# A decoder in one program: the convolution front reordered, with X fetched in parts and the last value tiles held elsewhere

## The reference, cut to what matters

```python
def conformer_conv(h, w_pw1, b_pw1, w_dw, b_dw, ln_g, ln_b, w_pw2, b_pw2):
    u = h @ w_pw1 + b_pw1                       # 1024 -> 2048
    a, gate = jnp.split(u, 2, axis=-1)
    u = a * jax.nn.sigmoid(gate)
    u = lax.conv_general_dilated(u, w_dw[:, None, :], window_strides=(1,),
        padding=((CONV_WIDTH - 1, 0),), feature_group_count=D_MODEL) + b_dw   # 31 taps, by channel
    u = jax.nn.silu(layer_norm(u, ln_g, ln_b))
    return u @ w_pw2 + b_pw2                    # 1024 -> 1024

h = rms_norm(x, norm_mix[0])
x = x + conformer_conv(h, ...)
x = x + memory_cross_attention(rms_norm(x, norm_mem[0]), mem, w_q, w_k, w_v, w_o)
x = x + swiglu(rms_norm(x, norm_ffn[0]), w_gate, w_up, w_down)
# then: a layer with differential attention (rotary tables from `positions`, and a factor
# lambda from four small vectors), the same memory attention and feed-forward part,
# and a hybrid layer with sparse and sliding-window attention and a convolved feed-forward part
```

## Time and profile before

| | us |
|---|---|
| timed runs: median of 3 (lowest to highest) | 1323.1 (1322.09 to 1323.24) |
| profiled execution: whole | 1318.42 |
| profiled execution: span of the core | 1316.0 |
| mean granted PE clock, share of full | 0.967 |
| PE busy | 1205.4 (92% of the span) |
| DVE busy | 913.8 (69%) |
| ACT busy | 598.1 (45%) |

### The profile page before, as it was taken

One profiled execution on the slowest core, in us unless ns is written; L12 is line 12 of the kernel. 1 busy time (PEld: TensorE's weight loads), 2 busy tenths in 40 slices (PEclk: granted clock), 3 DMA queues, 4 the chain that ended last, 5 costly groups with the idle time before them and its releaser, 6 DMA issues.

```text
span 1316.0 us, 24483 instructions
## 1 busy us (share of the span) xinstructions
PE 1205.4 (92%) x9162; PEld 1138.2 (86%) x9162; DVE 913.8 (69%) x1514; ACT 598.1 (45%) x1009; POOL 96.8 (7%) x76
## 2 busy tenths in 40 slices
PE   5899979999999999998999999998977796899995
PEld 5898878999999989778999999998955586899995
DVE  5987577676665687566767666558887358899855
ACT  4655354444444432344454444443255333566541
POOL 0457100000000000000000000011000001000000
PEclk9899999999999999999999999999989788899998
DMA  7334354245555545114515554553550021355551
GB/s 264 128 114 146 125 186 167 78 173 170 187 191 192 188 165 192 64 65 160 182 61 177 189 185 170 195 186 136 179 192 7 1 96 65 130 189 188 180 207 64
DMA packets 30631, 195.27 MB, mean 148 GB/s; under 512 B 3168, under 2 KB 7392, under 8 KB 7392
## 3 DMA queue, kind: packets, MB, share of 16 engines
q1 hardware_dynamic: 30560, 194.27, 42.2%
HBM read 193.21 MB, written 1.05 MB: 148 GB/s over the span
## 4 chain that ended last, share of the span: by engine, by line
PE 76%; DVE 13%; ACT 4%; issue 4%; DMA 1%; DVEq 0%; ACTq 0%; SPq 0%
PE acc L444 19%; PE acc L446 19%; PE acc L445 19%; PE acc L474 6%; DVE wlo L1172 3%; PE acc L460 2%; DVE wlo L1167 2%; PE acc L731 2%; ACT whi L845 2%; PE st L597 1%; PE sc L507 1%; PE sc L695 1%; DVE Hlo L1200 1%; PE tp L444 1%; DMA raw<-weights 1%
## 5 line engine op out<-in xcount | busy, mean ns | idle before, releaser
L444 PE MATMUL acc<-Hhi,whi 128*128 128x256 f32 x1376 | 396.5, 288 | 13.9 <-DVE wlo L1172 13.7
L445 PE MATMUL acc<-Hlo,whi 128*128 128x256 f32 x1376 | 391.9, 285 | 0.0
L446 PE MATMUL acc<-Hhi,wlo 128*128 128x256 f32 x1376 | 391.7, 285 | 0.0
L845 ACT ACTIVATE whi<-raw 128x1024 fp32r<-128x1024 f32 x164 | 173.2, 1056 | 412.4 <-PE acc L446 383.3
L1167 DVE TENSOR_TENSOR wlo<-raw,whi 128x1024 fp32r<-128x1024 f32 x164 | 205.6, 1254 | 118.8 <-ACT whi L845 118.8
L444 PEld LDWEIGHTS acc<-Hhi,whi 128*128 128x128 f32 x1376 | 266.8, 194 | 17.8 <-DVE wlo L1172 16.0
L445 PEld LDWEIGHTS acc<-Hlo,whi 128*128 128x128 f32 x1376 | 267.0, 194 | 1.6 <-issue 1.4
L446 PEld LDWEIGHTS acc<-Hhi,wlo 128*128 128x128 f32 x1376 | 266.7, 194 | 0.0
L444 PE MATMUL acc<-FH,whi 128*128 128x256 f32 x848 | 241.6, 285 | 19.8 <-DVE wlo L1172 13.8
L446 PE MATMUL acc<-FH,wlo 128*128 128x256 f32 x848 | 240.3, 283 | 0.0
L1172 DVE TENSOR_TENSOR wlo<-raw,whi 128x1024 fp32r<-128x1024 f32 x164 | 202.8, 1237 | 1.3
(11 more groups left out here) (255 smaller groups left out, 1739.7 us busy)
## 6 DMA issues: line engine op xcount, KB each, us to landing
raw<-weights SPq DMA_DIRECT2D x180, 1024.0 KB, 4.9
MEM<-mem_in SPq DMA_DIRECT2D x2, 1024.0 KB, 10.9
cst<-consts SPq DMA_DIRECT2D x1, 1126.0 KB, 12.3
X<-x_in SPq DMA_DIRECT2D x1, 1024.0 KB, 6.1
out<-X SPq DMA_DIRECT2D x4, 256.0 KB, 2.1
PT<-positions SPq DMA_DIRECT2D x1, 128.0 KB, 14.1
cst<-consts SPq DMA_DIRECT2D x1, 32.0 KB, 1.7
```

What stands on the lines that cost most here:

```text
L444: pe.matmul(dst, w, x, start=first, stop=False)
L445: pe.matmul(dst, w, xl, start=False, stop=False)
L446: return pe.matmul(dst, wl, x, start=False, stop=last)
L845: act.activation(whi[j][:, 0:HALF, :], raw[j][:, 0:HALF, :], ACT.Copy).then_inc(hi_out, 1)
```

## The change

- SP: X comes in four parts of 256 KB with a semaphore each; tile 0 comes in two halves (`head_loaded`, then `raw_loaded[0]`); `positions` is fetched before the memory.
- ACT: a one-element activation behind the gains comes first; X's high parts follow the parts of X. The squares of X are taken in four pieces behind tile 0's high part.
- PE: pairs 0 and 1 of X are multiplied with only the first half of tile 0's low part done (`lo_head`); the second half is waited for ahead of pair 2.
- mix0 and ln_var join the norms whose squares POOL adds; PE sums two chunks for them.
- The loops over pw1 on ACT and DVE are written out. DVE does the norm ahead of the split of tile 2, and the taps stand in portions of 6, 6 and 7 behind tiles, splits and gates.
- Value tiles 6 and 7 are loaded to `held`, in the memory of Hhi and Hlo, once pw1 is done. The first two tiles of pw2 are loaded behind value tiles 4 and 5 and split ahead of and behind the LayerNorm.
- PE's mean is summed in pieces between value tiles: chunks 0 to 4 behind value tile 2, 5 and 6 behind 3, 7 behind 4.
- Constants and lambda's sums move on DVE between the splits of tile 1 and the norm; lambda and the rope angles move behind the subtraction of the mean; the two Sin activations stand ahead of the Silu.

Cut to its core:

```diff
@@ -165,7 +165,9 @@
         wlo = [sb(f"wlo{j}", [P, KC, MB], F32R) for j in range(2)]
         X = sb("X", [P, DC, S])
         SQ = sb("SQ", [P, DC, S])
-        Hhi, Hlo = sb("Hhi", [P, DC, S], F32R), sb("Hlo", [P, DC, S], F32R)
+        with ExitStack() as shared:
+            Hhi, Hlo = sb("Hhi", [P, DC, S], F32R, shared), sb("Hlo", [P, DC, S], F32R, shared)
+        held = [sb(f"held{j}", [P, KC, MB]) for j in range(2)]
         with ExitStack() as shared:
             H2 = sb("H2", [P, 2, DC, S], F32R, shared)
         H2hi, H2lo = H2[:, 0, :, :], H2[:, 1, :, :]
...
-        SUMMED = ["mem0", "ffn0", "attn1", "mem1", "ffn1", "pre2", "fpre2"]
+        SUMMED = ["mix0", "ln_var", "mem0", "ffn0", "attn1", "mem1", "ffn1", "pre2", "fpre2"]
...
-            sp.dma_start(X[:, :, :], cols(x_in)).then_inc(x_loaded, 16)
-            for j in range(2):
-                sp.dma_start(raw[j][:, :, :], weights[j].rearrange("p (k m) -> p k m", k=KC)).then_inc(raw_loaded[j], 16)
+            tile_of = lambda t: weights[t].rearrange("p (k m) -> p k m", k=KC)
+            for p in range(4):
+                sp.dma_start(X[:, 2 * p:2 * p + 2, :], cols(x_in)[:, 2 * p:2 * p + 2, :]).then_inc(x_loaded[p], 16)
+            sp.dma_start(raw[0][:, 0:HALF, :], tile_of(0)[:, 0:HALF, :]).then_inc(head_loaded, 16)
+            sp.dma_start(raw[0][:, HALF:KC, :], tile_of(0)[:, HALF:KC, :]).then_inc(raw_loaded[0], 16)
+            sp.dma_start(raw[1][:, :, :], tile_of(1)).then_inc(raw_loaded[1], 16)
             sp.dma_start(cst[:, gains:NCONST], consts[:, gains:]).then_inc(cst_loaded, 16)
+            sp.dma_start(PT[:, 0, 0:S].bitcast(I32), positions.partition_broadcast(P)).then_inc(pos_loaded, 16)
             sp.dma_start(MEM[:, :, :], cols(mem_in)).then_inc(mem_loaded, 16)
-            sp.dma_start(PT[:, 0, 0:S].bitcast(I32), positions.partition_broadcast(P)).then_inc(pos_loaded, 16)
             def load(i, j):
-                sp.dma_start(raw[j][:, :, :], weights[bass.ds(2 * i + j, 1)].rearrange("o p (k m) -> p (o k) m", k=KC))\
-                    .then_inc(raw_loaded[j], 16)
+                t = tile_of(2 * i + j) if isinstance(i, int) else \
+                    weights[bass.ds(2 * i + j, 1)].rearrange("o p (k m) -> p (o k) m", k=KC)
+                sp.dma_start(raw[j][:, :, :], t).then_inc(raw_loaded[j], 16)
...
+            sp.wait_ge(tile_done, T0["pw1"] + 8)
+            for j in range(2):
+                sp.dma_start(held[j][:, :, :], tile_of(T0["memv"] + 6 + j)).then_inc(held_loaded[j], 16)
+            behind_whole(WHOLE0, WHOLE1 - 4)
+            for j in range(2):
+                sp.wait_ge(tile_done, T0["memv"] + 4 + j + 1)
+                sp.sem_inc(raw_loaded[j], 16)
+                load(WHOLE1 // 2, j)
...
+            def sum_squares(name):
+
+                sources = [SQ, SQF] if name == "pre2" else [SQ]
+                for p in range(1, 4):
+                    pool.wait_ge(s_sq, sq.at(SQ_OF[name], p + 1))
+                    for q in sources:
+                        ins = pool.tensor_tensor(out=q[:, 0:2, :], in0=q[:, 0:2, :], in1=q[:, 2 * p:2 * p + 2, :], op=ALU.add)
+                        if p < 3 or q is not sources[-1]:
+                            pc.link(ins)
+                ins.then_inc(squares_summed, 1)
+
+            sum_squares("mix0")
...
+                    if name == "pw1":
+                        pe.wait_ge(lo_head, 1)
+                    else:
+                        tile_in(L0[name])
                     if not norm_name:
                         pe.wait_ge(acc_free, G0[name] + 1)
                     if h.n[source] == 4:
                         for p in range(4):
                             pe.wait_ge(s_h, h.at(source, p + 1))
+                            if name == "pw1" and p == 2:
+                                tile_in(L0[name])
...
-            for k in (0, 1, 2, 3, 4):
+                whole(k % 2, "memv", 0, 8, k, turned=True, src=held[k % 2] if k >= 6 else None)
+
+            def mean_of(chunks):
+                for k in chunks:
+                    pe.wait_ge(conv_done, 1 + k + 1)
+                    mm = pe.matmul(st[:, 0:S], ones[:, :], UC[:, k, :], start=k == 0, stop=k == DC - 1)
+                return mm
+
+            for k in (0, 1, 2):
                 value_tile(k)
-            norm_stats("ln_mu", UC, lambda k: pe.wait_ge(conv_done, 1 + k + 1))
+            pe.wait_ge(st_used, N0["ln_mu"])
+            mean_of(range(5))
+            value_tile(3)
+            mean_of((5, 6))
+            value_tile(4)
+            mean_of((7,)).then_inc(stat_ready, 1)
             value_tile(5)
-            norm("ln_var", "ln")
+            pe.wait_ge(squares_summed, SUMMED.index("ln_var") + 1)
+            norm_stats("ln_var", chunks=2)
...
-            act.wait_ge(x_loaded, 16)
+            act.activation(rs[:, 0, 0:1], cst[:, 0:1], ACT.Copy)
             for p in range(4):
+                act.wait_ge(x_loaded[p], 16)
                 hi_scaled(pair(Hhi, 2 * p), pair(X, 2 * p), gcol("g_mix0"), 2 * p).then_inc(s_taken, 1)
-            split(16, 0)
-            act.activation(SQ[:, :, :], X[:, :, :], ACT.Square).then_inc(s_sq, 1)
+            act.wait_ge(head_loaded, 16)
+            act.activation(whi[0][:, 0:HALF, :], raw[0][:, 0:HALF, :], ACT.Copy).then_inc(hi_out, 1)
+            act.wait_ge(raw_loaded[0], 16)
+            act.activation(whi[0][:, HALF:KC, :], raw[0][:, HALF:KC, :], ACT.Copy).then_inc(hi_out, 1)
+            for p in range(4):
+                act.activation(pair(SQ, 2 * p), pair(X, 2 * p), ACT.Square).then_inc(s_sq, 1)
             split(16, 1)
             act.wait_ge(cst_loaded, 16)
+            act.wait_ge(s_given, given.at("lam"))
+            act.activation(lam[:, 2:4], lam[:, 0:2], ACT.Exp).then_inc(s_taken, 1)
...
+            ahead("pw1", 0, 8, 0)
+            ahead("pw1", 0, 8, 1)
+            gate(0)
+            ahead("pw1", 0, 8, 2)
+            conv_products(0, 0, 0)
+            ahead("pw1", 0, 8, 3)
+            gate(1)
+            conv_products(0, 0, 1)
+            ahead("pw1", 0, 8, 4)
+            conv_products(0, 1, 0)
+            ahead("pw1", 0, 8, 5)
+            gate(2)
+            conv_products(0, 1, 1)
+            conv_products(0, 2, 0)
+            gate(3)
+            conv_products(0, 2, 1)
...
+            pw2 = 16 * (T0["pw2"] // 2 + 1)
+            split(pw2, 0)
             value_tile(5)
+            act.wait_ge(s_given, given.at("rope"))
+            act.activation(rope_s[:, :], TG[:, 0, 0:S], ACT.Sin)
+            act.activation(rope_c[:, :], TG[:, 1, 0:S], ACT.Sin).then_inc(s_taken, 1)
...
-            ahead("memv", 0, 8, 6)
+            split(pw2, 1)
             value_tile(7)
-            ahead("memv", 0, 8, 7)
-
-            act.wait_ge(s_given, given.at("lam"))
-            act.activation(lam[:, 2:4], lam[:, 0:2], ACT.Exp).then_inc(s_taken, 1)
-            act.wait_ge(s_given, given.at("rope"))
-            act.activation(rope_s[:, :], TG[:, 0, 0:S], ACT.Sin)
-            act.activation(rope_c[:, :], TG[:, 1, 0:S], ACT.Sin).then_inc(s_taken, 1)
...
+            norm("mix0")
+            ahead("pw1", 0, 8, 0)
+            pw1_tile(0)
+            pw1_tile(1)
+            ahead("pw1", 0, 8, 1)
+            gated(0)
+            pw1_tile(2)
+            ahead("pw1", 0, 8, 2)
+            conv_taps(0, 0, 6)
+            pw1_tile(3)
+            ahead("pw1", 0, 8, 3)
+            gated(1)
+            conv_taps(0, 6, 12)
+            pw1_tile(4)
+            ahead("pw1", 0, 8, 4)
+            conv_taps(0, 12, DVE_TAPS)
+            conv_end(0)
+            pw1_tile(5)
+            ahead("pw1", 0, 8, 5)
+            gated(2)
+            conv_taps(1, 0, 6)
+            pw1_tile(6)
+            conv_taps(1, 6, 12)
+            pw1_tile(7)
+            conv_taps(1, 12, DVE_TAPS)
+            gated(3)
+            conv_end(1)
+            for c in range(2, DC):
+                conv_taps(c, 0, DVE_TAPS)
+                conv_end(c)
...
+            ahead("memv", 0, 8, 6)
+            norm("ln_var", LN_EPS)
+            for p in range(4):
+                dve.tensor_tensor(out=pair(UC, 2 * p), in0=pair(UC, 2 * p), in1=both(R[:, :]), op=ALU.mult).then_inc(s_given, 1)
+            for p in range(4):
+                dve.wait_ge(s_taken, taken.at("ln", p + 1))
+                dve.tensor_tensor(out=Olo[:, 2 * p:2 * p + 2, :], in0=SQ[:, 2 * p:2 * p + 2, :],
+                                  in1=f(Ohi[:, 2 * p:2 * p + 2, :]), op=ALU.subtract).then_inc(s_h, 1)
+            ahead("memv", 0, 8, 7)
```

186 lines of the change are left out of this document (77 added, 109 removed).

## The result

| | before | changed |
|---|---|---|
| timed, median of 4 (lowest to highest), us | 1323.14 (1322.09 to 1323.24) | 1306.99 (1305.47 to 1309.53) |
| profiled execution: whole / span, us | 1318.42 / 1316.0 | 1307.87 / 1306.1 |
| mean granted PE clock | 0.967 | 0.963 |
| first memory-query matmul, us | 196.54 | 180.22 |

A forecast was written before the change was run, and what follows sets the result against it. PE was busy 92% of the span; below 200 us it waited for DVE's order of work. Savings 4.3 + 2.4 + 4.4 + 2.4 + 3.3 + 4.8 = 21.6 us gave a forecast of 1301.5 us, range 1294 to 1309.

The forecast's parts named there:

- rival 1: Before pw2: LayerNorm's tail outlasts its cover, 3 us of wait and 1.8 at 1.2 GHz; 1306 us, chance 0.13.
- rival 2: pw1 stays DVE's: splits meet POOL, tiles 1 to 7 save only 1, statistic costs 1.5; 1306.5 us, chance 0.13.
- Rival 3: At the start, small transfers are served in turn, PE starts at 15.7; 1306.2 us, chance 0.08.
- rival 5: Loads past the held tiles come late, so pw2's weights do: 3.3 + 1.8 us back, 1306.5; chance 0.02.
- The front: Before PE's first matmul: X in parts and an early table load start PE at 11.0 instead of 15.34; 4.3 us.
- The first statistic: Sum of squares behind pw1's tile 0: POOL adds eight chunks to two, PE sums those without waiting; 2.4 us.
- Tiles 1 to 7: In pw1: DVE's new order shrinks 8.7 us of loss to 4.3, with stalls at tiles 2, 6, 7; 4.4 gained.
- Keys and values: Key and value tiles: two chunks instead of eight for the variance, convolution keeping ahead; 2.4 us gained, 87.5 long.
- Before pw2: Ahead of pw2: held value tiles let its weights load and split early, so no wait; 3.3 us gained.
- pw2: Second convolution projection: constants and tables moved away from it, 23.7 us instead of 28.5; 4.8 gained.
- rival 4: Whole kernel slower: denser work lowers PE's granted clock, 0.950 eats the gain, 0.945 gives 1330 us; chance 0.02.
- The footing: Whole time: the median of timed runs lies 4.7 us above the profiled execution, so 1296.8 becomes 1301.5.

The follow-up runs named there:

- warm: Changed kernel with 36 unused matmuls of ones by ones on PE ahead of its first; profiled execution 1309.91 us, first memory-query matmul at 179.10.
- no_held: Changed kernel with value tiles 6 and 7 from raw again, pw2's tiles loaded behind them and split behind the LayerNorm; profiled execution 1307.37 us.
- sq8: Changed kernel with PE summing all eight chunks of squares for mix0 again and POOL none; profiled execution 1312.06 us.
- pw2_turn: Changed kernel with pw2's first turn written out, its second tile's weights split ahead of the memory norm's Hlo and Hhi; profiled execution 1307.87 us.
- rope_early: Changed kernel with lambda and angles before DVE's mean wait, sines before value tile 4's copy, ACT's pw2 tile 1 split behind value tile 5; profiled 1304.44 us.
- best2: Changed kernel plus idle PE matmuls, tile 2 split before norm, later memory/position loads, earlier angles, pw2 turn reordered, DVE taps respread; median 1297.04 us, ratio 0.9799.

## Why the prediction was right, point by point

The range of 1294 to 1309 held, and "faster" was right. But the forecast of 1301.5 was 5.5 us too low, outside the range of 1297 to 1305 that its own case had, and by the number alone rivals 1, 2, 3 and 5 (1306 to 1306.5) lay nearer. None of them is what happened: the traces show the forecast's mechanisms, each stage a little dearer, and a part of rival 1. The landmark says where: M at 180.22 against 174.8 (151.1 + 23.7), 5.4 us.

- **The front: 3.3 us instead of 4.3.** X came no later than forecast, the weights did. The step that failed is "tile 0's first half (512 KB, 1.3 us behind X) has landed by then": the 1.3 us were reckoned at 408 GB/s, but the stretch moved 345, and ACT waited until 9.67. Rival 3, transfers in turn, would have had X at 10.4 and was wrong: X was scaled by 7.9. The Trainium skill ("DMA: Bandwidth & Descriptors", Anatomy of one DMA) gives a fixed cost of 2.0 us, fitted to transfers that GpSimd issues; these are issued by SP. Paid by each part in turn it would have had X land at 11.6, by the prediction's estimate. Here the parts took 2.9 to 4.1 us each and were issued 0.5 us apart, so whatever is fixed in them overlaps.
- **Tile 0: 8.51 us, taken as 7.1.** The largest error of the front, 1.4 us, and no term of the sum: "7.1" was the old stage's duration carried over. That stage had 2.7 us of matmuls 0.21 us apart (the pace of 1.2 GHz) before they came 0.12 apart; the changed kernel had 5.9. In warm, where PE had been at work before, tile 0 took 6.01 us, so the slow pace is the whole of the error. That this pace is the lower clock is read from no_held: from 157.78 to 162.85 its matmuls stood 0.21 us apart too, and there the granted clock is 0.50, that is 1.2 GHz.
- **The first statistic: 2.58, forecast 2.4.** Right, and shown alone by sq8. POOL was done at 17.97 and DVE at 19.05, by two halves of 1.78 and 2.30, where both had been put at 17.5; both lie before tile 0's end at 20.55. That cover was partly luck: it was so long because tile 0 was slow, and in warm it was gone.
- **Tiles 1 to 7: 45.46, forecast 44.7.** Waits at tiles 2, 6 and 7 were named at 1.9, 1.1 and 1.3 and came as 1.96, 1.57 and 0.66, in sum 4.2 where 4.3 was forecast. The 0.8 us lie in PE's own work, 41.3 us for seven tiles that were put at 5.76 each, 40.3; part of it is the matmul behind each wait. That the waits' sum came so near hides two errors that cancel: the wait at tile 6 was put 0.5 too short and the one at tile 7 0.6 too long. Behind the first stands a meeting that was too cheap: a gate of 0.88 took 2.41 beside POOL, a half split 2.32. No clock was charged behind the waits, and that held here; in pw2_turn the same wait of 1.95 was followed by a lower clock that cost 1.5 us. The meeting, DVE's rows first and then POOL's:

```profile
44.11 2.32 DVE L1231 TENSOR_TENSOR wlo<-raw,whi 128x1024 fp32r<-128x1024 f32 x1
46.35 2.41 DVE L1629 SCALAR_TENSOR_TENSOR A<-TG,cst,SG 128x256 f32<-128x256 f32 x2
...
45.42 1.60 POOL L448 TENSOR_TENSOR E<-SQ 128x256 f32<-128x256 f32 x1
46.99 1.49 POOL L444 TENSOR_TENSOR A<-A 128x512 f32<-128x512 f32 x1
```

- **Keys and values: 87.36, forecast 87.5.** No wait for conv_done.
- **Before pw2: no DVE wait, 0.27 of issue.** The held tiles did what was said, and no_held prices them at 5.7 us, with the lower clock behind the wait.
- **pw2: 25.90, forecast 23.7.** The mis-sized step, 2.2 us. Its slack was thin and on paper: "ACT splits tile 1 at 153 to 155, DVE ends it at 156.6" was 161.1. Of the 4.5 us, 3.2 are PE's own lateness (154.3 for 151.1). The mis-sized term is "lambda and the rope angles 4.4": they stood on DVE from 135.2 to 141.9, 6.7 us, for the cast and the scaling cost 1.07 and 1.32 beside POOL instead of 0.29 and 0.35. So the norm began 3.8 us after its statistic was ready. The tail behind the norm took the 9.2 that it was given, and the split behind the tail was 0.9 quicker than forecast. That was rival 1's mechanism at a smaller size, 0.9 at tile 1 instead of 3 ahead of tile 0, and rope_early removes it. At tile 3 "about 0.7" was 1.39, by an Hlo of 2.02 us (0.88 for the same pair at 164.11) beside POOL; pw2_turn, which puts the split ahead of it, removes it. The last 0.6 us are again PE's own work, 23.6 for the 23.0 of four tiles at 5.76.
- **The other rivals.** pw1 kept 3.6 of its 4.4 us and the statistic cost no wait (rival 2). The granted clock was 0.962 to 0.968 in the changed kernel's executions, against 0.967 in the profile of before and 0.959 to 0.966 in the executions of before beside the experiments, so rival 4's loss did not come. pw2's weights came early (rival 5).
- **The footing.** Adding 4.7 for the lucky profile was right: M moved by 16.3 and the medians by 16.1, while the two profiled spans differ by 9.9.

## What to carry to other kernels

Price a new order on the engine that is waited for by walking its list with durations from the trace; that came within 1 us for the seven tiles 1 to 7 of pw1. But price each instruction that meets another engine's at its contended duration, and a thin slack as spent. Put work that waits for nothing into the idle time ahead of a wait, not behind it, and judge a change of 1% by a landmark behind the last moved instruction, not by two profiled spans.

## What was not expected of the hardware

- PE's slow phase at its first matmuls differs from execution to execution. In ten profiles without warm's matmuls the pace changed from 0.21 to 0.12 us a matmul between 2.7 and 5.9 us after the first one, and tile 0 took 7.09 to 8.56 us. So up to 1.5 us of an earlier start can be given back. The profile's granted clock says 1.00 throughout; the pace says otherwise. With PE at work since 1.06 it was 0.12 from the second matmul on. The Trainium skill ("TensorE: Matmul & The Clock Gate", Part 1) calls this phase variable from run to run as well, and these runs agree.
- DVE instructions with one tensor input can suffer beside POOL too: a cast of 128x256 took 1.07 for 0.29 and a scaling 1.32 for 0.35. It is not so for every instruction there: seven taps at 54.02 took 2.83 us, their usual 0.40 each, while POOL was busy for 2.75 us of that stretch. So these two engines meet elsewhere than at semaphores, which the description ahead of the prediction leaves out. The Trainium skill ("SBUF — State Buffer", Who interferes with whom) names cast and tensor_scalar among the operations that can take the shared port, and the rows bear it out.
- The late attention is granted between 0.67 (best2) and 1.00 (before) of the clock in different executions of nearly the same instructions; between the profiles of before and changed that is some 4 of the 6.4 us (16.3 less 9.9) by which the spans fall short of the shift. What decides it was not tried.
